# A hybrid attention layer on one core: later second score visits, outputs before the next head's preparation, and an opening with four weight pieces in flight

## The reference, cut to what matters

```python
h = rmsnorm(x, norm_w[l])
proj = h @ w_in[l]
gq, gk, gv, gg, glr, hq, hf, hi, hg = jnp.split(proj, offsets, axis=-1)
...
o_intra = jnp.einsum('bhij,bhje->bhie', A, v_)
o_inter = jnp.einsum('bhid,bhde->bhie', q_ * jnp.exp(b), S)
S_new = jnp.exp(b_last)[..., 0, :, None] * S + jnp.einsum('bhjd,bhje->bhde', k_dec, v_)
...
o_a = head_rmsnorm(o_a, gla_norm_w[l]) * jax.nn.silu(gg.astype(jnp.float32))
mixed = jnp.concatenate([o_a, o_b], axis=-1).astype(x.dtype)
x = x + mixed @ w_out[l]
return rmsnorm(x, final_norm_w)
```

## Time and profile before

| | |
|---|---|
| time, median of 3 runs | 877.41 us (877.16 to 878.36) |
| the profiled execution | 877.31 us, of which the span from first to last instruction is 875.6 us |
| mean granted TensorE clock | 0.999 |
| TensorE busy | 855.6 us, 98% of the span |
| VectorE busy | 602.3 us, 69% |
| ScalarE busy | 413.1 us, 47% |
| GpSimd busy | 85.1 us, 10% |
| moved by DMA | 167.74 MB, mean 192 GB/s |

### The profile page before, as it was taken

How to read it: one execution, slowest core, us unless ns; L and a number is a source line. 1 busy time by engine, 2 the same in 40 slices (tenths; PEclk the granted TensorE clock), 3 DMA queues, 4 the chain that set the end, 5 groups by cost and what they waited for, 6 DMA issues and landing times.

```text
span 875.6 us, 13716 instructions
## 1 busy us (share of the span) xinstructions
PE 855.6 (98%) x5379; PEld 698.8 (80%) x5379; DVE 602.3 (69%) x982; ACT 413.1 (47%) x554; POOL 85.1 (10%) x128
## 2 busy tenths in 40 slices
PE   8999999999999999999999999999999999999996
PEld 5886888888888878888778778778788888888885
DVE  5723377753587747577887888889885678556756
ACT  6621442324445325273464655745555455335454
POOL 4010111110000001011111100000111100000000
PEclk9999999999999999999999999999999999999999
DMA  7386569989755846567776655545776988865654
GB/s 263 96 276 217 168 186 236 202 193 242 237 173 154 276 145 202 166 181 162 165 156 149 140 176 160 164 131 181 153 159 136 289 201 268 309 203 181 202 172 192
DMA packets 75170, 167.74 MB, mean 192 GB/s; under 512 B 7333, under 2 KB 15561, under 8 KB 73961
## 3 DMA queue, kind: packets, MB, share of 16 engines
q1 hardware_dynamic: 45266, 108.02, 37.4%
q0 software_dynamic: 16896, 50.34, 26.8%
q10 hardware_dynamic: 12952, 8.61, 3.5%
HBM read 158.56 MB, written 58.72 MB: 248 GB/s over the span
## 4 chain that ended last, share of the span: by engine, by line
PE 72%; DVE 16%; ACT 5%; issue 3%; DMA 3%; DVEq 1%; ACTq 0%
PE main L554 42%; PE main L805 8%; PE main L747 5%; PE sc L805 4%; DMA raw<-in_w_in 3%; DVE w_lo L1237 3%; PE po L805 2%; PE st L805 2%; DVE att L1348 1%; ACT w_hi L847 1%; PE sc L612 1%; PE sc L747 1%; PE po L640 1%; PE po L643 1%; PE st L625 1%
## 5 line engine op out<-in xcount | busy, mean ns | idle before, releaser
L554 PE MATMUL main<-h_hi,w_hi 128*128 128x512 f32 x640 | 256.6, 401 | 0.1
L554 PE MATMUL main<-h_hi,w_lo 128*128 128x512 f32 x640 | 250.0, 391 | 0.0
L554 PE MATMUL main<-h_lo,w_hi 128*128 128x512 f32 x640 | 249.6, 390 | 0.0
L1237 DVE TENSOR_TENSOR w_lo<-raw,w_hi 128x1024 fp32r<-128x1024 f32 x102 | 124.6, 1222 | 118.0 <-ACT w_hi L847 117.1
L847 ACT ACTIVATE w_hi<-raw 128x1024 fp32r<-128x1024 f32 x102 | 107.8, 1058 | 192.4 <-PE main L554 134.7
L554 PEld LDWEIGHTS main<-h_hi,w_lo 128*128 128x128 f32 x640 | 120.1, 188 | 26.0
L554 PEld LDWEIGHTS main<-h_hi,w_hi 128*128 128x128 f32 x640 | 120.2, 188 | 25.6 <-issue 0.5
L554 PEld LDWEIGHTS main<-h_lo,w_hi 128*128 128x128 f32 x640 | 120.4, 188 | 23.1
L868 ACT ACTIVATE ex<-ex 128x512 f32<-128x512 f32 (+2 forms) x84 | 52.4, 641 | 59.1 <-DVE ex L1377 49.2
L554 PE MATMUL main<-w_hi,h_hi 128*128 128x512 f32 x128 | 50.5, 395 | 0.3 <-DVE val L1491 0.3
L1708 DVE TENSOR_TENSOR w_lo<-feat,w_hi 128x1024 fp32r<-128x1024 f32 x26 | 31.8, 1224 | 27.4 <-ACT w_hi L1161 27.2
(11 more groups left out here) (307 smaller groups left out, 1494.1 us busy)
## 6 DMA issues: line engine op xcount, KB each, us to landing
raw<-in_w_in SPq DMA_DIRECT2D x104, 512.0 KB, 4.6
w_sum<-in_w_out POOLq DMA_DIRECT2D x48, 512.0 KB, 5.0
w_sum<-in_w_in POOLq DMA_DIRECT2D x24, 512.0 KB, 6.0
w_sum<-w_sum POOLq DMA_DIRECT2D x24, 512.0 KB, 5.4
raw<-w_sum SPq DMA_DIRECT2D x24, 512.0 KB, 3.5
feat<-w_sum SPq DMA_DIRECT2D x24, 512.0 KB, 3.5
raw<-in_w_out SPq DMA_DIRECT2D x14, 512.0 KB, 4.6
feat<-in_x SPq DMA_DIRECT2D x6, 1024.0 KB, 7.4
```

The costliest lines, as they stand in the source:

```text
L554: mm = pe.matmul(main[c][:, :], a, b, start=(k == 0 and j == 0), stop=(k == KT - 1 and j == 2))
L1237: dve.tensor_tensor(w_lo[:, q % SPL, :, :], raw[:, q % RAW, :, :], w_hi[:, q % SPL, :, :], ALU.subtract).then_inc(lo_ok, 1)
```

## The change

On TensorE the second visit moves one slot later in head 0, in the first head of the shared groups and in both heads of the pair groups; the state update moves two slots later in the first shared heads (the second update one slot) and in the pair groups; in the shared groups outputs and mean square of the first head move one slot later; in the pair groups the mean square of the first head moves one slot earlier. On VectorE both scalings of the second visit come before the state steps, the copies of the scores before the next head's running sum, and the cut of the outputs before the next head's preparation. On ScalarE the taking of the outputs comes before the next head's exponentials, except at the hand-over inside a shared group.

In the opening, x tile 0 is loaded and squared in two halves and its first normalisation is done in two parts; only the first half of `norm_w` is spread by TensorE, the second by a broadcast load; pieces 2 and 3 go to a place in `val` without waiting for the `raw` buffers, so that four pieces can be in flight, and pieces 4 and 5 wait for less. In group 0 VectorE takes the four banks before it splits the last piece. Seven filler transposes instead of four stand first.

```diff
@@ -387,9 +390,14 @@
                     n = first_piece(G) + p
                     s = p % RAW
                     last = QP if isinstance(G, int) and G == G_C and p < RAW else RAW
-                    if not (isinstance(n, int) and n < RAW):
-                        sp.wait_ge(lo_ok, n - last + 1)
+                    if not (isinstance(n, int) and n < 2 * RAW):
+                        early = RAW if isinstance(n, int) and n < 3 * RAW else 0
+                        sp.wait_ge(lo_ok, n - last - early + 1)
                     rows = src[p * PK * P:(p + 1) * PK * P, bass.ds(col, GW)]
+                    if isinstance(n, int) and RAW <= n < 2 * RAW:
+                        sp.dma_start(first_raw[:, s, :, :], rows.rearrange("(k p) n -> p k n", p=P)).then_inc(
+                            first_in[s], 16)
+                        continue
                     sp.dma_start(raw[:, s, :, :], rows.rearrange("(k p) n -> p k n", p=P)).then_inc(raw_in[s], 16)
 
             sp.dma_start(nrow, norm_w.rearrange("(o n) -> o n", o=1)).then_inc(nw_in, 16)
@@ -397,8 +405,11 @@
             def x_tile(t):
                 sp.dma_start(xin[:, t, :], x[t * P:(t + 1) * P, :]).then_inc(x_in[t], 16)
 
-            x_tile(0)
+            for a in range(2):
+                h = slice(a * D // 2, (a + 1) * D // 2)
+                sp.dma_start(xin[:, 0, h], x[0:P, h]).then_inc((x_left, x_in[0])[a], 16)
             group(w_in, C_GV, G_V, range(0, 2))
+            sp.dma_start(nwb[:, D // 2:], norm_w[D // 2:].partition_broadcast(P)).then_inc(nb_in, 16)
             x_tile(1)
             group(w_in, C_GV, G_V, range(2, 4))
             x_tile(2)
@@ -666,15 +677,18 @@
 
             pe.wait_ge(ones_ok, 1)
             pe.wait_ge(nw_in, 16)
-            for j in range(4):
+            for j in range(2):
                 pe.matmul(main[j][:, :], ones[0:1, :], nrow[:, j * 512:(j + 1) * 512], start=True,
                           stop=True).then_inc(nb_ps, 1)
             pe.wait_ge(consts, 1)
 
             def transposes(t, half):
 
-                pe.wait_ge(xn_ok, 2 * t + half + 1)
                 for j in (2 * half, 2 * half + 1):
+                    if t == 0 and j == 0:
+                        pe.wait_ge(xq_ok, 1)
+                    else:
+                        pe.wait_ge(xn_ok, 2 * t + half + 1)
                     if t:
                         pe.wait_ge(xt_lo, 4 * (t - 1) + j + 1)
                     for k in range(4 * j, 4 * j + 4):
...
@@ -769,9 +782,10 @@
                 return {z: a.get(z, []) + b.get(z, []) for z in a | b}
 
             alone = dict(T=7, L=[12, 12, 12, 16, 16], U=[13, 22], O=[19, 24], M=28)
-            shared = dict(T=0, L=[4, 4, 4, 8, 8], U=[3, 12], O=[11, 15], M=20)
+            shared = dict(T=0, L=[4, 4, 4, 9, 9], U=[5, 13], O=[12, 16], M=21)
             second = dict(T=17, L=[18, 21, 21, 25, 25], U=[20], O=[28], M=31)
             earlier = alone | dict(U=[13, 20], O=[19, 22], M=26)
+            alone |= dict(L=[12, 12, 12, 17, 17], O=[20, 24])
             group(G_C, False, head_tasks(gla_at(0) | alone))
             group(G_C + 1, False, head_tasks(gla_at(1) | earlier))
             for h in range(2):
@@ -782,8 +796,8 @@
                 todo = {}
                 for u in range(2):
                     z = 16 * u
-                    todo |= head_tasks(hg_at(m, u) | dict(T=z, L=[z + 4, z + 4, z + 4, z + 8, z + 8], U=[z + 3],
-                                                          O=[z + 11], M=z + 15 - u))
+                    todo |= head_tasks(hg_at(m, u) | dict(T=z, L=[z + 4, z + 4, z + 4, z + 9, z + 9], U=[z + 5],
+                                                          O=[z + 11], M=z + 14))
                 return todo
 
             with pe.Fori(0, 2) as i:
...
@@ -946,11 +962,15 @@
                     act.activation(h_hi[:, 4 * j:4 * j + 4, t * P:(t + 1) * P],
                                    side[j][:, :].rearrange("p (a n) -> p a n", a=4), ACT.Copy).then_inc(xt_hi, 1)
 
-            squares(0)
+            act.wait_ge(x_left, 16)
+            step(act.activation(junk[:, 0:D // 2], xin[:, 0, 0:D // 2], ACT.Square, accum_out=rs[:, 4:5]))
+            step(act.activation(rs[:, 4:5], rs[:, 4:5], ACT.Identity, bias=cst[:, 2:3], scale=1.0 / D))
+            act.wait_ge(x_in[0], 16)
+            step(act.activation(junk[:, 0:D // 2], xin[:, 0, D // 2:], ACT.Square, accum_out=rs[:, 0:1]))
+            step(act.activation(rs[:, 0:1], rs[:, 0:1], ACT.Sqrt, bias=rs[:, 4:5], scale=1.0 / D))
+            act.sem_inc(xss, 1)
             split(0, -3)
-            broadcast(2)
             highs(0, [0])
-            broadcast(3)
             split(0, -2)
             highs(0, [1])
             squares(1)
...
@@ -1092,11 +1112,11 @@
                 g, s = gla_head(2 + h), hg_head(0, h)
                 a, b = g["level"], s["level"]
                 nxt = gla_head(3) if h == 0 else hg_head(2, 0)
-                nxt = [nxt["decay"]] * h + [nxt["values"], nxt["early"]]
+                ready = [nxt["decay"]] * h + [nxt["values"]]
                 return {0: [g["quads"], g["keys"], a(3)], 1: [a(4), a(5)],
                         2: [s["decay"], s["values"], s["early"], g["take"](0)],
                         3: [g["take"](1)], 4: [s["quads"], s["keys"], b(3)], 5: [g["rstd"], b(4), b(5)],
-                        6: nxt + [s["take"](0)],
+                        6: ready + [s["take"](0), nxt["early"]],
                         "end": [lambda: act.preload_act_table_set(LNEXP)] * h + [s["rstd"]]}
 
             todo = gla_steps(0)
@@ -1118,7 +1138,8 @@
                     h, nxt, lv, z = hs[u], hs[u + 1:u + 2], hs[u]["level"], 4 * u
                     todo[z] = [h["quads"], h["keys"], lv(3)]
                     todo[z + 1] = [lv(4), lv(5)]
-                    todo[z + 2] = [f for x in nxt for f in (x["decay"], x["values"], x["early"])] + [h["take"](0)]
+                    todo[z + 2] = [f for x in nxt for f in (x["decay"], x["values"])] + [h["take"](0)] + [
+                        x["early"] for x in nxt]
                     if u == 0:
                         todo[z + 3] = [h["rstd"]]
                 todo["end"] = [lambda: act.preload_act_table_set(LNEXP), h["rstd"]]
...
@@ -1444,13 +1469,14 @@
             dve.tensor_copy(ones_r[:, :], ones).then_inc(onesr_ok, 1)
 
 
-            def normalise(t, half):
-                h = slice(half * D // 2, (half + 1) * D // 2)
-                if half == 0:
+            def normalise(t, half, cols=slice(0, D // 2)):
+                h = slice(half * D // 2 + cols.start, half * D // 2 + cols.stop)
+                if half == 0 and cols.start == 0:
                     dve.wait_ge(xss, t + 1)
                     step(dve.reciprocal(rs[:, t:t + 1], rs[:, t:t + 1]))
                 dve.scalar_tensor_tensor(out=xin[:, t, h], in0=xin[:, t, h], scalar=rs[:, t:t + 1], in1=nwb[:, h],
-                                         op0=ALU.mult, op1=ALU.mult).then_inc(xn_ok, 1)
+                                         op0=ALU.mult, op1=ALU.mult).then_inc(
+                                             xn_ok if cols.stop == D // 2 else xq_ok, 1)
 
             def lows(t, js=range(4)):
                 for j in js:
...
@@ -1491,7 +1518,7 @@
                     dve.tensor_copy(val[:, c, bass.ds(half * GW, GW)], main[c][:, :]).then_inc(free[c], 1)
                 return f
 
-            group(0, {}, values(0), 1)
+            group(0, {}, values(0), 1, NP - 1)
 
             dve.wait_ge(par_ps, 1)
             step(dve.tensor_copy(par[:, :], po[:, 0:R_END]))
@@ -1610,7 +1637,7 @@
                 g = gla_head(h)
                 ar, sl, cp = g["arg"], g["scale"], g["scores"]
                 todo = {0: [g["args"], g["ends"]] * (h > 0) + [g["early"]], 1: [g["quads"], ar(4), sl(3), ar(5)],
-                        2: [cp(0), cp(1), cp(2), sl(4), g["states"](0), sl(5)],
+                        2: [cp(0), cp(1), cp(2), sl(4), sl(5), g["states"](0)],
                         3: [cp(3), cp(4)], 5: [g["states"](1), g["cut"]], 7: [g["norm"]]}
                 if nxt:
                     todo[6] = [f for x in nxt for f in (x["args"], x["ends"])]
@@ -1624,11 +1651,11 @@
                 ar, sl, cp = g["arg"], g["scale"], g["scores"]
                 ar2, sl2, cp2 = s["arg"], s["scale"], s["scores"]
                 return {0: [g["quads"], ar(4), sl(3), ar(5)],
-                        1: [cp(0), cp(1), cp(2), sl(4), g["states"](0), sl(5)],
-                        2: [s["args"], cp(3), cp(4), s["ends"]], 3: [g["states"](1), s["early"], g["cut"]],
+                        1: [cp(0), cp(1), cp(2), sl(4), sl(5), g["states"](0)],
+                        2: [cp(3), cp(4), s["args"], s["ends"]], 3: [g["states"](1), s["early"], g["cut"]],
                         4: [s["quads"], ar2(4), cp2(0), sl2(3), ar2(5)],
-                        5: [cp2(1), cp2(2), sl2(4), s["states"](0), sl2(5), g["norm"]],
```

(9 more changed lines are left out.)

47 lines of the change are left out of this document (29 added, 18 removed).

## The result

The changed kernel takes 881.39 us (median of 19 runs, 876.63 to 883.07; mean 880.34), the kernel before beside it 877.55 us (median of 20, 876.69 to 878.36; mean 877.60). The ratio, which is that of the means, is 1.0031 with an interval of 1.0019 to 1.0043: slower, by 0.3% in the mean and 0.4% in the median, outside the forecast range and on the side that I had given 0.15. (One further run, disturbed, of 1139.7 us at a clock of 0.71 is left out; with it the median is 881.52.)

A forecast was written before the change was run, and what follows sets the result against it. TensorE, busy in 98% of the span, was taken as the bound; removed waits and an earlier opening against new group-end stops summed to -1.2 us, from 877.3 to 876.1 us, range 868 to 880.

The forecast's parts named there:

- the clock falls in the stops: Rival, chance 0.10: TensorE's clock drops in the new stops of 2.4, 3.3 and 3.3 us, costing 4.5 us: 880.6 us.
- What bounds it: TensorE works in 98% of the span; gains come only from small holes, losses from new ones; VectorE has 0.3 us spare.
- Opening, -1.7: Start of the kernel: x tile 1 normalised at 15.3 us instead of 17.03, saving 1.7 us.
- the freed bank, -0.3: Group after the opening: VectorE copies the banks out before splitting the last piece, removing a 0.3 us wait.
- Tile 1 lands at 12.6: Opening: x tile 1, landing at 11.2 us before, lands 1.4 us later behind the added nwb load.
- The 1.4 us for the nwb load: Opening: the added 512 KB broadcast load ahead of x tile 1 delays it 1.4 us, at most 1.9.
- Second visits -6.4: Second visits to the scores: all five waits for scaled queries go, 5.9 us plus five refills of 0.1.
- state update -1.3: Pairs and first shared heads: waits for transposed keys in three pair heads go, 0.4 us plus three refills of 0.3.
- mean squares -2.8: Mean-square products on TensorE: four waits go, 1.7 us plus four refills of 0.27.
- Stops +6.6, +2.4, +1.0: Group ends: banks come free late, stopping TensorE 3.3 us behind two pair groups, 2.4 and 1.0 us behind shared groups.
- Behind the stops +1.1 and +0.2: After the shared stop a late quad scaling costs 1.1 us; in the group before, a late piece load costs 0.2.
- The stops are small: Rival, chance 0.25: the preparation does not push the groups' ends, so the stops go: 864.8 us, or 870.5 with half.

The follow-up runs named there:

- experiment 9: Kernel before with only the new opening (x tile 0 in halves, four weight pieces asked for at once, new transfer order): 876.75 us, ratio 0.9984.
- experiment 11: Kernel before with the new opening, but x tile 1 asked for ahead of the norm weight's right half: 876.23 us, ratio 0.9985.
- the heads alone: Changed kernel with the opening of the kernel before, so only the slots and orders of the heads change: 882.27 us, ratio 1.0048.
- experiment 1: Changed kernel with unneeded identity transposes on TensorE filling the four new stops at the groups' ends: 877.22 us, ratio 0.9996.
- experiment 7: Kernel of experiment 4 with the cut in the middle of the next head's preparation and banks freed before the last split behind pairs: 871.08 us, ratio 0.9921.
- experiment 8: Kernel of experiment 7 with ScalarE storing the four banks ahead of its last split at the end of the shared groups: 870.82 us, ratio 0.992.
- experiment 6: Kernel of experiment 5 with VectorE freeing the banks behind a pair before it splits the last weight piece: 878.39 us, ratio 1.0007.
- experiment 4: Changed kernel, but each group's last head has its outputs taken and cut behind the next head's preparation, as in the kernel before: 874.49 us, ratio 0.9963.
- experiment 5: Kernel of experiment 4 with the mean square of each group's last head moved to slot 1 of the next group: 880.69 us, ratio 1.0036.

## Why the prediction was wrong

The picture was right, the likeliest case was not: the rival "the clock falls in the stops" came true, and I had given it 0.10.

**What bounds it.** Right. That VectorE had 0.3 us to spare at a group's end was the number on which all hung.

**Opening, -1.7, and the freed bank, -0.3.** Too large: together 0.98 us (experiment 9). A step that failed is "Tile 1 lands at 12.6": it landed at 13.9. It was issued 1.3 us later (3.96 against 2.62) and took 9.9 us where it had taken 8.6. The 1.4 us for the nwb load were about right: with that load behind it (experiment 11) the tile is issued at 3.10, takes 8.9 us and lands at 12.0, 1.9 us sooner (1.4 against the opening alone, 13.4). What I left out is that it lands at 12.0 and not at 11.2 even then, half a microsecond of it because tile 0 is now two loads and stands longer at the issue. But the landing is not the whole of it: in experiment 11 the tile is normalised at 15.5, nearly the forecast 15.3, and the kernel gains 1.2 us and not 2.0. Some of the lead is lost again at the first head's transposes: 1.04 us ahead at the second group (65.85 against 66.89), 0.64 at those transposes (292.42 against 293.06), where a wait of 0.36 for VectorE's keys is new. Single traces tell such leads only roughly: with the same opening the second group starts at 65.3 to 66.1, and with the old one at 66.3 in the heads alone.

**Second visits -6.4, state update -1.3, mean squares -2.8.** Right, in the trace. From the start of the product ahead of each second visit to that of the product behind it, the twelve of them take 14.2 us where they took 20.6.

**Stops +6.6, +2.4, +1.0.** Right in kind and place; measured 3.27 twice, 2.0 and 0.6, so 9.2 for 10.0.

**Behind the stops +1.1 and +0.2.** Neither came in the changed kernel's trace: the first visit behind the shared stop at 509.45 waits for nothing. The slow products there hid a little of it: with the clock kept up (experiment 1) that visit waits 0.3.

**The sum without a drop of the clock.** By the starts in the trace: lead at the first head -0.6, waits removed with their refills -10.4, stops with theirs +9.8, together -1.2, as forecast (the opening's loss made up by the smaller stops and the missing wait). The profiled run less its 3.1 us of slow clock would be 876.5. The five runs at 0.997 or more lie around 877.1, only 0.45 below the kernel before, the fastest at 876.63; experiment 1 at -0.5. Some 0.7 us stay unexplained. These runs lie in the range.

**The clock.** This is the step that failed, and that moved the time out of the range: the sum has no term for it, it got a chance of 0.10, and the reading behind that was "Against: the three idle microseconds at 1.00". The last product of the kernel before is this:

```profile
868.05 0.28 PE L805 MATMUL st<-w_hi,h_lo 128*128 128x256 f32 x1
```

So TensorE had stood for 5.1 us when the clock fell, at 873.4. That is one stop, and one outcome. At the same place in the fourteen profiled runs the clock fell between 1.9 us (experiments 7 and 8) and 5.1 us (kernel before, experiment 6) behind the end of the last product, and stops of 2.0 to 3.3 us lie inside that spread. One row at 1.00 could not show that a stop of 3.3 us is safe. The price was near: 4.5 us forecast for all stops, 4.2 measured between the medians of experiment 1 and the changed kernel (2.9 between the means, since five of its 19 runs show no loss). It was near partly by luck: I let the clock stay down for as long as the stop had lasted, but the stop of 2.0 us cost 1.7 us and the second of 3.27 nothing. The Trainium skill's rule ("TensorE: Matmul & The Clock Gate", section "Why this matters for your kernels") says that an idle gap between bursts of matmuls puts the engine back to its lower level. The trace agrees behind two of its three long stops (0.50 behind those of 2.0 and 3.27 us), but not each time: the second stop of 3.27 us left the clock at 1.00.

**"The stops are small"**, 0.25, did not come true: the banks came free by the chain of the earlier trace rows.

## What to carry to other kernels

A wait removed in the middle of a group is won only if the engine that ends the group's chain is earlier too; otherwise it is lent, and comes back at the next thing that this engine owes (experiments 4 and 5). The gain of experiment 7 came from handing results over in the order in which the bounding engine asks for them: the cut when it can be made, then the banks, and last the split that nobody wants yet. A new stop of TensorE of two to three microseconds is not to be counted at its length alone: in the profile each of two drops of the clock cost 1.4 to 1.7 us of work, and 14 of the 19 runs read a mean clock as low as this one with its two drops, or lower. Where a stop can't be avoided, work that nobody needs can fill it (experiment 1). And where the runs of one program fall into bands, the granted clock beside each time is the first thing to look at.
